# A feed-forward layer in split fp32: up product by seven block products instead of eight, from the second round on

## The reference, cut to what matters

```
D_MODEL = 1024; SEQ = 1024; D_FF = 4 * D_MODEL
v = rmsnorm(h, mlp_norm_g[l])
hid = jnp.square(jax.nn.relu(jnp.einsum('bsd,df->bsf', v, w_up[l])))
h = h + jnp.einsum('bsf,fd->bsd', hid, w_down[l])
```

## Time and profile before

| what | us |
|---|---|
| median of 3 runs (range) | 3667.03 (3666.77 to 3667.93) |
| span of the profiled execution | 3664.2 |
| feed-forward units after the first, 698.76 to 1385.86 in the trace | 687.10 |

### The profile page before, as it was taken

How to read it: one execution, slowest core, us unless ns; L and a number is a source line. 1 busy time by engine, 2 the same in 40 slices (tenths; PEclk the granted TensorE clock), 3 DMA queues, 4 the chain that set the end, 5 groups by cost and what they waited for, 6 DMA issues and landing times. The chain is left out here.

```text
span 3664.2 us, 48293 instructions
## 1 busy us (share of the span) xinstructions
PE 3551.3 (97%) x17345; PEld 2912.5 (79%) x17345; DVE 1807.2 (49%) x3390; ACT 1233.6 (34%) x2310; POOL 1349.3 (37%) x783
## 2 busy tenths in 40 slices
PE   7999999999999999999999999999899999999999
PEld 6777777888888887788888888887688877777787
DVE  7665552444434345666666666666514243332422
ACT  4776442200000013455545555555301202020311
POOL 3222102333333331665565656654332222213432
PEclk9999999999999999999999999999999999999999
DMA  3011002211111103223322222311412111202242
GB/s 104 24 29 30 24 15 92 70 47 51 46 47 52 52 24 93 50 50 52 55 49 47 37 41 38 36 38 49 151 57 101 46 59 36 66 29 71 75 161 75
DMA packets 205189, 207.74 MB, mean 57 GB/s; under 512 B 15760, under 2 KB 160703, under 8 KB 205007
## 3 DMA queue, kind: packets, MB, share of 16 engines
q1 hardware_dynamic: 185438, 155.50, 17.2%
q10 hardware_dynamic: 19568, 49.63, 3.8%
HBM read 173.57 MB, written 31.52 MB: 56 GB/s over the span
## 5 line engine op out<-in xcount | busy, mean ns | idle before, releaser
L728 PE MATMUL ps<-all_u_hi,kept_w_hi 128*128 128x512 f32 x2016 | 814.2, 404 | 8.4 <-ACT residual L1125 4.1
L732 PE MATMUL ps<-all_u_hi,kept_w_lo 128*128 128x512 f32 x2016 | 789.1, 391 | 0.0
L731 PE MATMUL ps<-all_u_lo,kept_w_hi 128*128 128x512 f32 x2016 | 787.3, 391 | 0.0
L678 POOL CAST kept_w_hi<-kept_w_raw 128x1024 fp32r<-128x1024 f32 x116 | 127.8, 1102 | 1169.0 <-PE ps L728 691.4
L1544 POOL TENSOR_SCALAR even_probs<-even_probs,even_stat 128x640 f32<-128x640 f32 (+1 forms) x250 | 428.1, 1718 | 339.2 <-DVE even_stat L1991 339.2
L728 PEld LDWEIGHTS ps<-all_u_hi,kept_w_hi 128*128 128x128 f32 x2016 | 381.3, 189 | 79.6 <-ACT residual L1125 5.3
L732 PEld LDWEIGHTS ps<-all_u_hi,kept_w_lo 128*128 128x128 f32 x2016 | 379.1, 188 | 82.3
L731 PEld LDWEIGHTS ps<-all_u_lo,kept_w_hi 128*128 128x128 f32 x2016 | 380.9, 189 | 67.8
L1807 ACT ACTIVATE even_probs<-even_probs,even_stat 128x128 f32<-128x128 f32 (+7 forms) x256 | 199.2, 778 | 301.9 <-DVE even_stat L1985 301.9
L680 POOL TENSOR_TENSOR kept_w_lo<-kept_w_raw,kept_w_hi 128x1024 fp32r<-128x1024 f32 x116 | 282.7, 2437 | 9.3
L728 PE MATMUL ps<-kept_w_hi,all_u_hi 128*128 128x512 f32 x640 | 253.1, 396 | 10.4 <-DVEq L2897 7.2
(11 more groups left out here) (397 smaller groups left out, 6977.6 us busy)
## 6 DMA issues: line engine op xcount, KB each, us to landing
kept_w_raw<-in_even_w_in_dram SPq DMA_DIRECT2D x64, 512.0 KB, 6.7
kept_w_raw<-in_odd_w_in_dram SPq DMA_DIRECT2D x48, 512.0 KB, 3.7
kept_w_raw<-in_w_up_dram SPq DMA_DIRECT2D x16, 512.0 KB, 4.0
mlp_w_raw<-in_w_up_dram SPq DMA_DIRECT2D x16, 512.0 KB, 4.0
kept_w_raw<-in_w_down_dram SPq DMA_DIRECT2D x16, 512.0 KB, 3.6
mlp_w_raw<-in_w_down_dram SPq DMA_DIRECT2D x16, 512.0 KB, 3.6
scratch_h<-residual SPq DMA_DIRECT2D x8, 1024.0 KB, 4.9
residual<-scratch_negc ACTq DMA_DIRECT2D x16, 512.0 KB, 6.3
```

The lines of the kernel that those rows point to most:

```text
L678: nc.gpsimd.tensor_copy(hi, raw).then_inc(w_hi.sem, 1)
L728: ins = nc.tensor.matmul(dst, lh, rh, start=first, stop=False)
L731: nc.tensor.matmul(dst, lh, rl, start=False, stop=False)
L732: return nc.tensor.matmul(dst, ll, rh, start=False, stop=last)
```

## The change

From the second round on, the up product of two hidden tiles (a pair) is done as a 2 by 2 block product: the weights of the pair in four blocks A11, A12, A21, A22 (128 hidden by 512 input channels each, "halves" of a unit), the input in four blocks B11 to B22 (512 input channels by 512 tokens). Strassen's scheme needs seven block products M1 to M7 instead of eight, on sums of blocks. A block product is 4 channel tiles of three matmuls, 12 matmuls.

- PE: in rounds 2 to 8 a pair takes 7 x 12 = 84 matmuls where it took 96. The first round keeps 24 matmuls to a bank. M6 and M7 add onto banks that hold M3 and M4.
- POOL: works in halves of 128x512. In a pair it makes five sums of raw weight blocks (into `mlp_w_sum`) and splits seven blocks; in the down part it splits 8 halves. `slot(j)` has 7 places for split halves, and before it overwrites one, POOL waits `half_free`, which PE counts up when it begins the following half. There are now two raw slots; SP loads unit v when unit v - 2 is split, and in a pair both units stay until M7 is split.
- DVE, first round: besides its relus it makes 20 sums of input blocks ("quarters"), three dependent instructions each in PSUM, and after ACT's high part the low part. Twelve are made in the up part (`EARLY_AT`), in banks 6 and 7; PE waits for them (`quarter_ready.at(EARLY_SUMS)`) at the third token tile of the down part. Eight are made between the residual adds of the first down part, one after every second add.
- DVE and ACT, later rounds: the banks are combined into the four results (`blocks_out`): ACT copies three banks and does relu, square and high part for four results, DVE does six combinations and four low parts.
- The root of the norm is left out of the hidden values; its square scales the down sums, in the residual add (`ROOT_SQUARE`). So the spreading of the root (L538, L562, L608 in this stage) goes.
- `dynamic_dma_scratch_size=1024` is passed to the program's builder. No transfer in the page comes from POOL's queue.

The core of the diff:

```diff
+        EARLY_SUMS = 3 * HK
+        EARLY_AT = [range(3 * n // 2, 3 * (n + 1) // 2) for n in range(8)]
+        def place(j):
+            it = 0 if j < FIRST_HALVES else 1 + (j - FIRST_HALVES) // EACH
+            return (j + min(it, 5)) % 7
...
             @block.sync
+                def load(v):
+                    if v == 2:
+                        sp.wait_ge(w_lo.sem, w_lo.at(w.slots + 1))
+                    else:
+                        sp.wait_ge(half_ready.sem, half_ready.at(unit_ends(v - 2) - 1))
+                    for dst, src in unit(v // per, v % per)(w.raw[:, v % 2, :]):
+                        sp.dma_start(dst, src).then_inc(w_raw[v % 2].sem, 16)
...
             @block.gpsimd
+                def split(j, src):
+                    hi, lo = slot(j)
+                    before = held_before(j)
+                    if before is not None:
+                        pool.wait_ge(half_free.sem, half_free.at(before + 1))
+                    nc.gpsimd.tensor_copy(hi, src).then_inc(half_hi.sem, 1)
+                    pool.wait_ge(half_hi.sem, half_hi.at(j - 1))
+                    nc.gpsimd.tensor_tensor(lo, src, hi.bitcast(F32), ALU.subtract).then_inc(half_ready.sem, 1)
...
+                        split_sum(j + M1, A11, A22, ALU.add)
+                        split_sum(j + M5, A11, A12, ALU.add)
+                        split(j + M3, A11)
+                        split_sum(j + M2, A21, A22, ALU.add)
+                        split(j + M4, A22)
+                        split_sum(j + M6, A21, A11, ALU.subtract)
+                        split_sum(j + M7, A12, A22, ALU.subtract)
...
             @block.tensor
+                    def block_product(m, bank, onto=False):
+                        half_arrived(j + m)
+                        for k in range(HK):
+                            last = product(ps[:, bank, :], tile(j + m, k), ROWS_OF[m][k], k == 0 and not onto,
+                                           k == HK - 1, frees=k == 0, onto=onto)
+                        last.then_inc(block_done.sem, 1)
...
+                                    if it + half + t0 + i == 0 and t == 2:
+                                        pe.wait_ge(quarter_ready.sem, quarter_ready.at(EARLY_SUMS))
+                                    frees = t == t0 and (t0 == 4 and k > 0 or t0 == 0 and i == 0)
...
             @block.vector
+                def add(it, half, t):
+                    dve.wait_ge(pv_done.sem, pv_done.at(16 * it + half * TT + t + 1))
+                    v = h[:, t, half * HALF:(half + 1) * HALF]
+                    nc.vector.scalar_tensor_tensor(out=v, in0=ps[:, 4 + t % 4, :], scalar=ROOT_SQUARE[:, t:t + 1], in1=v,
+                                                   op0=ALU.mult, op1=ALU.add).then_inc(added.sem, 1)
...
+                for n in range(8):
+                    relu(n)
+                    quarters(EARLY_AT[n])
+                    low(0, n, n % 3, n // 2, n % 2)
+                for m in range(2 * TT):
+                    add(0, m // TT, m % TT)
+                    if m % 2 == 0:
+                        quarters(range(EARLY_SUMS + m // 2, EARLY_SUMS + m // 2 + 1))
...
-    nc = _bacc.Bacc("TRN2", target_bir_lowering=False, num_devices=1)
+    nc = _bacc.Bacc("TRN2", target_bir_lowering=False, num_devices=1, dynamic_dma_scratch_size=1024)
```

More of the change, by code:

```diff
@@ L559, in turn_act @@
                 .then_inc(hi_done.sem, 1)
+        if not spread:
+            return
         act.wait_ge(spread_done.sem, spread_done.at(1))
@@ L3082, in _ @@
-                turn_ident(ps[:, 0, 0:P], 34)
+                first_round()
+                down_round(0)
+                for it in range(1, rounds):
+                    for p in range(PAIRS_):
+                        blocks(it, p)
+                    down_round(it)
+                nc.tensor.transpose(ps[:, 0, 0:P], ident[:], ident[:]).then_inc(half_free.sem, 1)
+                turn_ident(ps[:, 0, 0:P], 33)
             @block.scalar
             def _(act):
-                turn_act(act, GAIN_MLP)
+                steps = [0]
@@ new lines, in quarter_low, with quarters @@
+                def quarter_low(i):
+                    out = SUMS[i][3]
+                    dve.wait_ge(quarter_sum.sem, quarter_sum.at(i + 1))
+                    dve.wait_ge(quarter_hi.sem, quarter_hi.at(i + 1))
+                    nc.vector.tensor_tensor(out[1], sum_bank(i), out[0].bitcast(F32), ALU.subtract)\
+                        .then_inc(quarter_ready.sem, 1)
+                def quarters(which):
+                    for i in which:
+                        quarter(i)
+                        if i not in (0, EARLY_SUMS):
+                            quarter_low(i - 1)
+                        if i == EARLY_SUMS - 1:
+                            quarter_low(i)
@@ L3154, in _ @@
+                quarter_low(len(SUMS) - 1)
+                for it in range(1, rounds):
+                    for p in range(PAIRS_):
+                        blocks_out(it, p)
+                    if it == rounds - 1:
+                        dve.wait_ge(gain_out.sem, gain_out.at(1))
+                    for m in range(2 * TT):
+                        add(it, m // TT, m % TT)
+                        if it == rounds - 1 and m >= RING:
+                            scaled_square(m - RING)
                 for m in range(2 * TT - RING, 2 * TT):
@@ L3155, in _ @@
                     scaled_square(m)
-        w_close(w, rounds, per)
-        turn_close()
+        w_lo.close(w.slots + 1)
+        w_hi.close(1)
+        for s in range(w.slots):
+            w_raw[s].close(rounds * per // 2 * 16)
+        turn_close(spread=False)
         gain_in.close(16)
```

425 lines of the change are left out of this document (304 added, 121 removed).

## The result

The changed kernel took 3699.23 us (median of 4, 3698.63 to 3701.77), the kernel before 3667.48 on the same chip: ratio 1.0083, 95% interval 1.0071 to 1.0096, 31.8 us slower. I had forecast 3676.6 with a range of 3650 to 3692.

What follows compares the result with a forecast made beforehand. PE was taken as the bound, busy 97% of 3664.2 us at 2.4 GHz. Terms -38.1 - 1.3 + 25.7 + 23.3 = +9.6 on the 3667.0 median gave 3676.6 us, range 3650 to 3692.

Steps and rivals of the forecast that it cites:

- the sum: All terms added over the whole kernel: +9.6 us on the kernel before, giving 3676.6 us.
- Fewer matmuls: PE, rounds 2 to 8: 24 matmuls a round fewer in seven rounds, all on the path, 38.1 us less.
- No spreading: Stage start: without spreading the root, PE's next matmul may start 1.71 us earlier; POOL's first splits leave a gain of 1.3.
- DVE in the first round: First round's down part: PE waits for DVE's sums, 10.5 us at the third tile, 13.2 at groups, 2.0 at M3; 25.7.
- POOL's supply: Rounds 2 to 8: POOL's split halves reach PE late at D0 and D3, 4.1 us in five rounds, 1.4 in two; 23.3.
- just in time: Rounds 2 to 6, up part: POOL's split for M7 was to be ready as PE wants it, with no wait.
- The sum from the Trainium skill's figure: POOL's price for 512 columns from the skill's 2048-column add: 1.38 us, making the forecast sum some 9 us longer.
- The port: DVE and POOL block each other on SBUF: DVE's low parts cost POOL's chain to D0 some 1.6 us a round.
- What costs nothing: Later rounds: ACT's copies, DVE's combinations, the scaled add, the gain load and smaller scratch were to add no time.
- The scaled add: DVE's residual add in the down part, scaled by the root's square: claimed no longer than the plain add.
- The gain load: Last round: issued after the last block, the load was to have 8.8 us until the first add, so cost nothing.
- Rival D: DVE's and POOL's waits both dearer, 34 and 40 us, port as lock at each low part: +35, 3702 us; chance 0.11.

Runs made afterwards that it cites:

- final2: final with DVE's wait for the last round's squared gain row moved from ahead of the first add to four adds later; 3647.45 us.
- final: Changed kernel with DVE's first-round quarter sums spread (8 before the third down tile, 12 between groups of four adds), three raw buffers and six places; 3647.01 us.
- raw3: Changed kernel with three raw weight buffers instead of two, six places of split halves instead of seven, and no shift of places; 3670.01 us.
- shift0: Changed kernel with places of split halves no longer shifting by one each round (half j always in place j modulo 7); 3686.82 us.
- fill: Changed kernel with PE's idle time at waits filled with small identity transposes that nobody reads, all waits kept; 3688.33 us.
- finalp: final with the six places renumbered so that the stage's last two split halves lie in the extra places, not the kept ones; 3648.15 us.

## Why the prediction was wrong

The direction was right and the size was not: the sum said +9.6, the span grew by 33.7. Step by step:

- *Fewer matmuls, -38.1.* Right: 3070 to 2902 in the stage.
- *No spreading, -1.3.* -1.7 for the spread, +1.0 for a hole at 699.87 (POOL's first splits were 2.3 apart, not 1.94): -0.7.
- *DVE in the first round, +25.7.* Measured 22.4 (8.0 at the third tile, 10.5 forecast; then 3.5 to 4.1 at the three groups, 2.3 at M3). Right within 3. PE was on again at 742.0, the very time worked out, but that is in part luck: in this trace all of the stage lies 1.8 later than in the trace before, so DVE was 2 sooner than forecast, and PE came to the tile at 734.0, not 731.5. DVE's steps cost 0.86 and 0.70 where I had 0.6 to 0.72 and port waits apart.
- *POOL's supply, +23.3.* Mechanism and place right, size 6.5 short: 29.8 measured (5.4, 5.1, 4.6, 4.2, 4.9 in rounds 2 to 6, 2.8 in 7 and 8). Round 3 shows where. PE begins D7 for its last four tiles at 893.11. The first pair's last block is split 9.9 later (9.5 forecast), the load takes 6.2 (6.1), the second pair 23.2 (21.1), D0's load 3.9 (3.8), its split and PE's restart 2.4 (2.3): PE begins D0 at 938.76, 45.7 after D7, where the forecast had 42.8 and 1.6 for the port. So the pair is what was too cheap. An undisturbed sum and split takes 3.65 (818.43 to 822.08) and not 3.47, since POOL idles 0.18 to 0.19 between them: 0.9 for the five of a pair. It shows as a new hole of 0.9 at M7 in rounds 3 to 6, where the forecast had "just in time". In round 2 D0's load also held POOL 5.7, not 3.8. The addition is 1.33 on the mean and the casts 0.66 to 0.72, with 1.31 and 0.61 forecast; alone, POOL's rows have 1.29 and 0.61. The sum from the Trainium skill's figure (GPSIMD Engine Reference, Elementwise — side-by-side cycle accounting), some 9 us more, comes near the measured wait, but for another reason: the line from that figure puts 512 columns at 1.38, above the 1.33 of this trace.
- *The port.* A hid low part takes 1.02 on the mean where 0.69 was its length alone. The one below begins 0.04 after a sum of POOL and takes 1.80. The rule of the Trainium skill (SBUF — State Buffer, Who interferes with whom) and the rows agree. The port is on the path through POOL: in the pair of round 3, four of its instructions (0.83, 1.07, 1.52, 1.62) are 0.2 to 0.5 longer than their like, 1.2 together, and D0's cast 0.4; the forecast had 1.6.

```profile
912.92 1.29 POOL L3142 TENSOR_TENSOR mlp_w_sum<-kept_w_raw 128x512 f32<-128x512 f32 x1 [0.18 <-POOL mlp_more_lo L3136]
912.96 1.80 DVE L3380 TENSOR_TENSOR mlp_hid_lo<-all_roots_spread,mlp_hid_hi 128x512 fp32r<-128x512 f32 x1
```

- *What costs nothing.* ACT's copies and DVE's combinations: right. The scaled add: no, it takes 0.75 (L3392) where the plain one took 0.69 (L3141 of the kernel before, median), part of DVE's term. The gain load: a hole of 1.5 us in the last round, behind the 9.9 that DVE stood for it. Two more of 0.5 there are the adds' own (final2).
- *The failed step is the sum itself.* It priced every hole at its own length and put the clock behind the holes at nothing, without a reason. "At a granted clock at its upper level, 2.4 GHz, in all 40 slices" was read from the kernel before and carried over to a kernel in which PE stands idle over 50 us more. The reading was too broad as well: a digit 9 in a slice means 90% or more, and just behind the stage the kernel before has 3.4 us at 0.50 where PE had stood 2.1 (rows below). In the changed kernel the clock at 0.50 for 30.7 us behind the holes cost 13.4 us by its length outside the holes, 13.8 against final, where no stretch at 0.50 is left (slow 17.9 to 4.1), and 11.4 in the stage when the idle time was filled. The first matmuls behind a wait, each some 0.1 longer, add about 3 to it. With these 16.7 and POOL's 6.5 the sum is +9.6 + 16.7 + 6.5 + 1.5 (gain) + 0.6 (start) - 3.3 (DVE) = +31.6, of 31.4 measured in the stage.

```profile
1391.87 5.35 PE L527 MATMUL ps<-all_ident,residual 128*128 128x128 f32 x32 [2.14 <-PEq L2994]
```
```profile
1392.90:1396.30 3.40, 3.40 (x19) 0.50 0.60 195
```

Rival D gave nearly the measured time (3702) for a wrong reason: it had 34 for DVE and 40 for POOL, where 22.4 and 29.8 were measured, and nothing for the clock.

## What to carry to other kernels

Where a change leaves TensorE idle that was never idle, price each hole by its length and ask for the clock behind it: here 55 us of holes came with 17 us of slow matmuls, some 13 of them by the lower clock. A supplier that was busy 56 us of a round of 87 (896.00 to 983.30) was late by 4 to 5, because its next load was issued only when its last buffer came free; one buffer more for raw data was worth more than one more for finished data (20 us of stage, raw3 against shift0). After a repair read also what follows the stage: one numbering of the places cost 5 us in the closing of it, and the other took as much back inside it.

## What was not expected of the hardware

- In the changed kernel the clock at 0.50 came in stretches of 3.4 or 6.8 us, behind holes of 8.0 and 5.0 us twice as long as behind those of 2.5 to 3.4. In shift0 one of 6.8 us began behind a hole of 2.0 (at 770.3, with one of 2.2 inside it), so the length of the hole does not settle it. Holes of one length differ: 3.36 us lowered the clock at 1026.0 and 1114.0 and not at 938.8 or 1201.8. Why is open; no kernel here tells it apart.
- In fill, identity transposes of 0.11 us whose result nobody reads were enough to keep the clock at 1.00 over the stage.
- DVE's squares beside POOL's split of 1024 columns took up to 2.82 us instead of 0.68 in final; that fell away with the places of finalp.
